# A keyed-expert stage: products of 512 columns, modulation sums moved to GpSimd, weights stored tile by tile

## What is computed

```
mod = jax.nn.silu(c) @ ada_w[l] + ada_b[l]
sh1, sc1, g1, sh2, sc2, g2 = jnp.split(mod[:, None, :], 6, axis=-1)
```

## Time and profile before

| | us |
|---|---|
| median of 3 runs (2588.99 to 2591.70) | 2591.24 |
| the profiled execution, its own time | 2591.11 |
| its span in the trace | 2589.3 |
| TensorE busy in the span | 2547.6 (98%) |
| VectorE busy | 1985.1 (77%) |
| ScalarE busy | 1426.9 (55%) |
| GpSimd busy | 0.2 (4 instructions) |

### The profile page before, as it was taken

How to read it: one execution, slowest core, us unless ns; L and a number is a source line. 1 busy time by engine, 2 the same in 40 slices (tenths; PEclk the granted TensorE clock), 3 DMA queues, 4 the chain that set the end, 5 groups by cost and what they waited for, 6 DMA issues and landing times. The chain is left out here.

```text
span 2589.3 us, 41783 instructions
## 1 busy us (share of the span) xinstructions
PE 2547.6 (98%) x14614; PEld 2210.2 (85%) x14614; DVE 1985.1 (77%) x2776; ACT 1426.9 (55%) x1835; POOL 0.2 (0%) x4
## 2 busy tenths in 40 slices
PE   9999999999999999999999999999999999999998
PEld 5798889897898888888889998878888888888887
DVE  6688378996787777776856645568988889898897
ACT  4654243484544444444544434457777777776775
POOL 0000000000000000000000000000000000000000
PEclk9999999999999999999999999999999999999999
DMA  8423345425787878786434555259999999999996
GB/s 340 159 98 105 116 131 169 137 81 188 242 312 282 299 280 278 249 297 203 154 113 141 184 181 170 97 210 381 343 349 351 349 360 347 361 356 344 353 357 225
DMA packets 223747, 627.19 MB, mean 242 GB/s; under 512 B 15344, under 2 KB 23568, under 8 KB 223376
## 3 DMA queue, kind: packets, MB, share of 16 engines
q1 hardware_dynamic: 223632, 625.64, 69.2%
HBM read 619.29 MB, written 6.29 MB: 242 GB/s over the span
## 5 line engine op out<-in xcount | busy, mean ns | idle before, releaser
L3870 DVE TENSOR_TENSOR wide_low<-wide,wide_high 128x2048 fp32r<-128x2048 f32 x288 | 657.4, 2288 | 97.8 <-ACT wide_high L3745 95.9
L3745 ACT ACTIVATE wide_high<-wide 128x2048 fp32r<-128x2048 f32 x288 | 552.5, 1919 | 210.3 <-PE bank L3597 104.4
L232 DVE TENSOR_TENSOR expert_tile_low<-slot,expert_tile_high 128x1024 fp32r<-128x1024 f32 x216 | 263.6, 1223 | 119.9 <-ACT expert_tile_high L224 119.9
L224 ACT ACTIVATE expert_tile_high<-slot 128x1024 fp32r<-128x1024 f32 x216 | 227.3, 1054 | 182.2 <-PE bank L242 65.7
L3593 PE MATMUL bank<-wide_high,xg_high 128*128 128x512 f32 x768 | 302.8, 394 | 0.1
L3594 PE MATMUL bank<-wide_high,xg_low 128*128 128x512 f32 x768 | 299.5, 390 | 0.0
L3597 PE MATMUL bank<-wide_low,xg_high 128*128 128x512 f32 x768 | 205.6, 389 | 0.0
L241 PE MATMUL bank<-h_high,expert_tile_high 128*128 128x256 f32 x704 | 173.4, 284 | 0.0
L242 PE MATMUL bank<-h_low,expert_tile_high 128*128 128x256 f32 x704 | 172.6, 283 | 0.0
L3597 PEld LDWEIGHTS bank<-wide_low,xg_high 128*128 128x128 f32 x768 | 144.1, 188 | 30.4
L3593 PEld LDWEIGHTS bank<-wide_high,xg_high 128*128 128x128 f32 x768 | 144.3, 188 | 29.4 <-DVE xg_low L3822 0.9
(11 more groups left out here) (611 smaller groups left out, 5133.4 us busy)
## 6 DMA issues: line engine op xcount, KB each, us to landing
wide<-in_moe_gu SPq DMA_DIRECT2D x192, 1024.0 KB, 6.4
wide<-in_moe_d SPq DMA_DIRECT2D x96, 1024.0 KB, 7.0
slot<-in_peer_u SPq DMA_DIRECT2D x128, 512.0 KB, 4.4
slot<-in_peer_v SPq DMA_DIRECT2D x128, 512.0 KB, 4.5
slot<-in_w_in SPq DMA_DIRECT2D x72, 512.0 KB, 3.6
picked_or_ada<-in_ada_w SPq DMA_DIRECT2D x48, 512.0 KB, 5.1
ada_slot<-in_ada_w SPq DMA_DIRECT2D x48, 512.0 KB, 4.7
slot<-in_ffn_gu SPq DMA_DIRECT2D x48, 512.0 KB, 3.6
```

Source lines behind the costliest of these rows:

```text
L224: core.nc.scalar.activation(self.tile_hi[:, place % 2], core.slot[u][:], ACT.Copy).then_inc(self.hi_ready.sem, 1)
L232: core.nc.vector.tensor_tensor(self.tile_lo[:, place % 2], slot[:], self.tile_hi[:, place % 2].bitcast(F32), ALU.subtract)\
L3745: nc.scalar.activation(w_hi[n % NB][:].rearrange("p c n -> p (c n)"), wide[n % U][:], ACT.Copy).then_inc(hi_ready.sem, 1)
L3870: nc.vector.tensor_tensor(w_lo[n % NB][:].rearrange("p c n -> p (c n)"), wide[n % U][:], w_hi[n % NB][:].rearrange("p c n -> p (c n)").bit ...
```

## The change

1. `Split` puts h's high and low parts side by side, so that for each block of 128 rows the 256 high columns and the 256 low ones are one run of 512.
2. A new `products_of_both` has 8 products of the high tile with these 512 columns and 8 of the low tile with the 256 high ones. A bank then holds two sums of 256 columns which somebody has to add. It is used for u's tiles in `experts` and for the gate and up tiles in `feed_forward`.
3. In `experts` VectorE adds the two halves (`sum_halves`, a reduce of 128x512 into `act_g`), once for each tile of u, and the gelu then reads `act_g` in place of the bank.
4. `add_tile` goes from VectorE to GpSimd as two instructions: `tensor_scalar` of the landed tile in place, and `tensor_tensor` that adds it to the sums (the first tile of a strip has only the `tensor_scalar`). There are two sums in turn, and four landing places in place of two. `add_rows` comes up to two rounds after the strip's last tile.
5. `weights` is laid out as [partition, tile, token]. What is used up of it makes the room for two of the landing places and for the second sums. `weigh` then reads 256 values in a run; the copy in `spread_weights` reads its bank with a stride and writes runs of 4.
6. In `feed_forward` VectorE adds the halves of every gate and up bank (two more reduces for a pair of tiles), and multiplies out of memory in place of the bank.

```diff
-        self.high, self.low = (core.sb(ctx, f"{name}_{part}", [P, C, n], F32R) for part in ("high", "low"))
+        self.parts = core.sb(ctx, f"{name}_parts", [P, C, 2, n], F32R)
+        self.high, self.low = self.parts[:, :, 0, :], self.parts[:, :, 1, :]
...
+    def products_of_both(self, pe, place, i, bank, split):
+        nc = self.core.nc
+        pe.wait_ge(self.hi_ready.sem, self.hi_ready.at(place + 1) + i * 4)
+        for c in range(C):
+            last = nc.tensor.matmul(bank[:, 0:2 * N], self.tile_hi[:, place % 2, c, :], split.parts[:, c].rearrange("p a n -> p (a n)"),
+                                    start=(c == 0), stop=False, skip_group_check=True)
+        last.then_inc(self.hi_used.sem, 1)
+        pe.wait_ge(self.lo_ready.sem, self.lo_ready.at(place + 3) + i * 4)
+        for c in range(C):
+            last = nc.tensor.matmul(bank[:, 0:N], self.tile_lo[:, place % 2, c, :], split.high[:, c, :], start=False, stop=(c == C - 1),
+                                    skip_group_check=True)
+        last.then_inc(self.core.tiles_used.sem, 1)
...
-            weights = core.sb(cg, "weights", [P, N, P])
+            weights = core.sb(cg, "weights", [P, P, N])
...
-                nc.scalar.activation(weights[:, q * B:q * B + B, :], core.bank[k % W][:, :].rearrange("p (b n) -> p b n", n=P), ACT.Copy)\
+                nc.scalar.activation(weights[:, :, q * B:q * B + B], core.bank[k % W][:, :].rearrange("p (b n) -> p n b", n=P), ACT.Copy)\
...
+    SLOTS = 4
-    slots = (side, core.sb(ctx, "ada_slot", [P, D]))
-    acc = core.sb(ctx, "ada_sums", [P, D])
+    slots = (side, core.sb(ctx, "ada_slot_1", [P, D]), within(0, "ada_slot_2", [P, D]), within(4, "ada_slot_3", [P, D]))
+    acc = (core.sb(ctx, "ada_sums_0", [P, D]), within(8, "ada_sums_1", [P, D]))
...
-                    if t >= 2:
-                        sp.wait_ge(summed.sem, summed.at(t - 1))
-                    if t > 1 and t % C == 1:
-                        sp.wait_ge(column.sem, column.at(t // C))
-                    sp.dma_start(slots[t % 2][:], ada[t]).then_inc(side_landed[t % 2].sem, 16)
+                    if t >= SLOTS:
+                        sp.wait_ge(summed.sem, summed.at(t - SLOTS + 1))
+                    sp.dma_start(slots[t % SLOTS][:], ada[t]).then_inc(side_landed[t % SLOTS].sem, 16)
...
-                halver.products(pe, place, i, lambda c: core.bank[w][:, 0:N], lambda c: split.high[:, c, :], lambda c: split.low[:, c, :])
+                halver.products_of_both(pe, place, i, core.bank[w], split)
...
+            sum_round = lambda t: t // 3 if t < 3 * THREES else (t - THREES) // 2
+            rows_due = {sum_round(g * C + C - 1) + 2: g for g in range(S)}
...
-            def add_tile(t, g=0):
...
+            def sum_halves(w, j, k):
+                dve.wait_ge(used.sem, used.at(E + k) + j * 4)
+                nc.vector.tensor_reduce(act_g[:, w, :], core.bank[w][:, :].rearrange("p (a n) -> p n a", a=2), AX.X, ALU.add).then_inc(u_summed.sem, 1)
+
+            def round_(j):
                 for w in range(2):
                     dve.wait_ge(geled.sem, geled.at(w + 2) + j * 2)
                     weigh(w, E + w, act_g[:, w, :], j * 2 + (E + w), j * 2)
-                    if tiles[w]:
-                        add_tile(tiles[w][0], g)
                     dve.wait_ge(used.sem, used.at(E + 2 * w - 1) + j * 4)
                     act_to_low(w, E + w, j * 2)
                     lower(2 + 2 * w, j + B0)
-                    if len(tiles[w]) == 2:
-                        add_tile(tiles[w][1], g)
+                    sum_halves(1 - w, j, 2 * w + 2)
                     lower(3 + 2 * w, j + B0)
...
+        @block.gpsimd
+        def _(pool):
+            for t in range(SIDE):
+                g, c, w = t // C, t % C, t % SLOTS
+                pool.wait_ge(side_landed[w].sem, side_landed[w].at((16 * (GROUPS // 2) if w < 2 else 0) + 16 * (t // SLOTS + 1)))
+                if c == 0:
+                    if g >= 2:
+                        pool.wait_ge(column.sem, column.at(g - 1))
+                    ins = nc.gpsimd.tensor_scalar(acc[g % 2][:], slots[w][:], core.c2s[:, c, :], None, ALU.mult)
+                else:
+                    nc.gpsimd.tensor_scalar(slots[w][:], slots[w][:], core.c2s[:, c, :], None, ALU.mult).then_inc(scaled.sem, 1)
+                    pool.wait_ge(scaled.sem, scaled.at(t - g))
+                    pool.wait_ge(summed.sem, summed.at(t))
+                    ins = nc.gpsimd.tensor_tensor(acc[g % 2][:], slots[w][:], acc[g % 2][:], ALU.add)
+                ins.then_inc(summed.sem, 1)
```

More of the change, by code:

```diff
@@ L1621, in retrieval @@
                     spread_weights(core, c2, a, h, picked, side[:, 3 * N:4 * N], weights, stage, early)
-            experts(core, cg, a, weights, split, side, early)
+            experts(core, cg, a, weights, split, side, early, within)
         core.release("keys_loaded", "keys_scored", "choose_vector_steps", "choice_exp", "choice_ready", "choice_turned", "choice_kept", "scores_kept",
@@ L2003, in zero_banks, with experts @@
         core.nc.tensor.matmul(core.bank[b][:, :].rearrange("p (o n) -> p o n", o=4), core.zeros[:], core.zeros[:].rearrange("p (o n) -> p o n", o=1).broadcast_to([P, 4, P]), start=True, stop=False, skip_group_check=True)
-def experts(core, ctx, a, weights, split, side, early):
+def experts(core, ctx, a, weights, split, side, early, within):
     nc = core.nc
     E = EARLY
+    SLOTS = 4
     act_g = core.sb(ctx, "act_g", [P, 2, N])
@@ L2023, in experts @@
     halver = Halver(core, ctx, "expert")
-    side_landed = [core.count(f"ada_landed_{w}") for w in range(2)]
+    side_landed = [core.count(f"ada_landed_{w}") for w in range(SLOTS)]
+    u_summed, scaled = core.count("expert_halves_summed"), core.count("ada_rows_scaled")
     stored = [core.count(f"early_stored_{k}") for k in range(STAGES)]
@@ L2116, in add_rows @@
             def add_rows(g):
-                pe.wait_ge(summed.sem, summed.at(C) + g * C)
+                pe.wait_ge(summed.sem, summed.at(C * g + C))
                 if g == 0:
@@ L2163, in _ @@
             dot(E, 0, 0)
-            for j in range(THREES):
-                round_(j, rows_in(j))
-            for j in range(THREES, PAIRS - 1):
-                k = j - THREES
-                round_(j, (k // 4 + (3 * THREES // C - 1), None) if k % 4 == 0 and k <= TWOS else (None, None))
+            for j in range(PAIRS - 1):
+                round_(j)
             turn_rows()
@@ L2251, in weigh @@
                 dve.wait_ge(weighed.sem, weighed.at(n - 1) + i) if not isinstance(n, int) or n >= 2 else None
-                row = weights[:, :, bass.ds(tile, 1)].rearrange("p t o -> p (t o)")
+                row = weights[:, bass.ds(tile, 1), :].rearrange("p o t -> p (o t)")
                 nc.vector.tensor_tensor(act_g[:, w, :], source, row, ALU.mult).then_inc(weigh_steps.sem, 1)
@@ L3378, in gate_and_up @@
                         pe.wait_ge(free.sem, free.at(u // 2 + 1) + i * 2)
-                    halver.products(pe, u, i, lambda c: core.bank[u][:, 0:N], lambda c: split.high[:, c, :], lambda c: split.low[:, c, :])
+                    halver.products_of_both(pe, u, i, core.bank[u], split)
             def down_part(i, u):
@@ L3442, in round_ @@
                     halver.lower(dve, place + u, i)
+                    if u == 0 and before is not None:
+                        gate_sum(1, before)
                     if u == 1 and before is not None:
                         hidden(1, before)
+                    if u == 2 and here:
+                        gate_sum(0, i)
                     if u == 3 and here:
@@ L3483, in feed_forward @@
     rescaled.passed(3)
+    for count in (gate_summed, hid_high):
+        count.passed(FT - 2)
     halver.passed(U * R, False)
```

129 lines of the change are left out of this document (62 added, 67 removed).

## The result

The changed kernel takes 2692.62 us (median of 4 runs, 2691.24 to 2694.86), the kernel before 2590.11 on the same chip (4 runs, 2587.68 to 2591.7): a ratio of 1.0392, interval 1.0380 to 1.0405. It is slower by 102.5 us. The prediction was 2710.

The account below looks back on a forecast made before the run. TensorE was taken as the bound, busy 2547.6 of 2589.3 us. To 2591.1 came +90.2 and +52.8 for GpSimd's turns, -0.6, -9.7, -10.8, +0.5 and -3.1: +119.3, so 2710 us, range 2568 to 2800.

Parts of the forecast that it names:

- Wide products: TensorE's products of u, gate and up: 0.07 us gained a tile, 6.2 on 88 tiles, 3.1 in the feed-forward part.
- Adding the halves: VectorE's reduces, 0.69 us each: hidden in the rounds and feed-forward part, 0.5 us later at the end.
- Weights tile by tile: Strided copy out of a bank before the rounds: taken as no cost, at most 23.7 us; `weigh` 0.42 for 0.62.
- Landing places: Four places for modulation tiles: the first 16 rounds' 9.7 us of gaps go; SyncE's queue now waits for sums.
- The sums on GpSimd: GpSimd's price for a modulation tile: scaling 1.5 us, addition 2.22, together 3.44; ends 1.82 and 4.16.
- One at a time: In the rounds, GpSimd and VectorE's two-input instructions (3.28 us a half) exclude each other: 2710 us, chance 0.62.
- The sum: Half a round of `experts` takes 8.44 us with three tiles (+90.2 in all), 6.72 with two (+52.8).
- The rule of turns: In the rounds, VectorE's 3.28 us of two-input instructions and GpSimd's tile work add up in each half.
- The signs it named: Profile signs in the rounds: L233 lengthened from 1.21 us, TensorE waiting for `act_lo`, or GpSimd over 3.7 us a tile.
- the slow rival: In the rounds, no mutual blocking, but GpSimd's 4.16 us a tile delays SyncE's queue: 2589.8 us; 0.09 with slow copies.
- side by side, but GpSimd is slow: Three-tile rounds take 12.5 us for 11.24 through SyncE's queue, +19.8: 2589.8 us; chance 0.09 shared with slow copies.

Follow-up runs that it names:

- e6_on_vector_narrow: Changed kernel with the sums back on VectorE and u's high products narrow again (16 of 256 columns): 2583.47 us, ratio 0.9969.
- e5_on_vector: Changed kernel with the modulation's sums back on VectorE as one fused instruction a tile, the rest kept: 2569.13 us, ratio 0.9915.
- e7_on_vector_two: Changed kernel with the sums back on VectorE and two landing places in place of four: 2570.29 us, ratio 0.9917.
- e3_add_only: Changed kernel with GpSimd's addition in full, its scaling on one column, first tiles filled: 2733.15 us with a ninth round, stage 563.6.
- e2_scale_only: Changed kernel with GpSimd's scaling in full and its addition on one column: 2570.47 us, ratio 0.9918, stage 503.8.
- e8_two_scalings: Changed kernel with a second full scaling on GpSimd in place of the addition: 2661.06 us, ratio 1.0276, stage 590.9.
- e1_tiny: Changed kernel with GpSimd's scaling and addition on one column, first tiles filled: 2677.36 us with a ninth round, stage 503.5.

## Why the prediction was nearly right, and where it was not

The time, 2692.6, lies 17 us under the forecast and in its range, the sign was the likeliest one, and the place (the rounds, L233 and `act_lo` lengthened, 1.21 and 0.41 us as their shortest) was named. But two of its steps were off in opposite directions, and the nearness is luck in that part: with the prices that GpSimd really has, its own rule gives 2854 us, above its range of 2568 to 2800.

- **Wide products**: right mechanism, size a little low. A half of a round went from 5.62 to 5.51 us (predicted 5.55), a feed-forward tile from 2.88 to 2.79. With `e6_on_vector_narrow` the two are worth 14.3 us together; 9.3 had been put down.
- **Adding the halves**: right. The reduces take 0.68 us (L2277, L3465) against 0.69 predicted from L3215, and the part after the stage became 2.9 us shorter, so they are hidden there.
- **Weights tile by tile**: right. The strided copy takes 596 ns (L1971) where it took 597, and `weigh` 0.42 us where nothing disturbs it (`e5_on_vector`).
- **Landing places**: the gaps are gone as predicted, in `e5_on_vector` the clock is 1.00 from 715 on and TensorE busy 284.3 of 285 us. The cause was named wrongly: with two places all but some 3 us of the gain stays (`e7_on_vector_two`). By the traces it is rather the sums in tiles of their own, which is not shown. The wait that comes in, SyncE's for the sums, is there with 251.4 us, and it is the main path of the loss: TensorE waits 60.4 us for tiles against 20.2 for `act_lo`. The prediction named this path, but its sum priced only VectorE's turns.
- **The sums on GpSimd**: the mis-sized term. The addition takes 2.34 at its shortest and 2.44 on the mean against 2.22. The scaling takes 2.84 at its shortest and 3.75 on the mean, against 1.5 chosen and 2.22 as the upper end: the bound itself was wrong. It was taken from instructions of VectorE, as if GpSimd at its slowest needed no more for one input than VectorE for two. A tile is 6.2 us, not 3.44. The Trainium skill, GPSIMD Engine Reference, section Engine selection, gives about twice VectorE's time for two inputs and roughly line-rate for one. For two inputs this trace agrees, 2.40 against 1.22 us. For one it does not: 2.84 against 0.75 us (L2283 before), so the measurement decides.
- **One at a time**: half right. For additions it holds: 3.02 for 1.22 us, 2.34 for 0.42, and 60 us when they stand alone (`e3_add_only`). For scalings it holds in part. A scaling waits, at its start, for a VectorE instruction that is under way (4.08 us in place of 2.84 in the period shown, 1.24 for a single column), and holds VectorE's two-input ones for 0.97 us (`e2_scale_only`). In its last 1.88 us they run in their normal time. This is also where the 0.69 us of `act_lo` in that period come from: the scaling ends at 1121.79, its last 1.88 us begin at 1119.91, and 0.42 later, at 1120.33, `act_lo` ends. The Trainium skill, SBUF — State Buffer, section Who interferes with whom, calls it an exclusive lock, which whoever issues first has for the whole instruction. The additions (2.34 us for 0.42) agree with it, the scalings (0.97 of 2.85 us) do not.
- **The sum**: 8.44 and 6.72 us were predicted for a half with three and two tiles in its round; measured are 8.06 (720.89 to 978.87, 32 halves) and 6.58 (to 1294.49, 48 halves). The rule of turns with the true prices, 2.84 + 7/8 x 2.40 = 4.94 us a tile, would have given 3.28 + 1.5 x 4.94 = 10.7 and 8.2 us, a time of 2854 with the other terms as they stood. The price too low and the rule too wide cancelled.
- **The signs it named**: two of them came together. L233 has a mean of 1508 ns, the sign for one at a time, and GpSimd needs 5.4 us for a tile in the rounds with three (258.0 / 48), with SyncE waiting for sums, the sign for the slow rival.
- **The rival "side by side, but GpSimd is slow"** had the mechanism that does most: its limit of 3.70 us for a tile in a round of three, passed through SyncE's queue. At the 564 us of work measured it gives 564 - 455 = 109 of the 120 us by which the changed kernel's stage exceeds that of `e5_on_vector`; GpSimd's waits for VectorE are in these 564 us. It came out at 2589.8 because its highest price for a tile, 4.16 us, had the same too low bound in it.

What is shown: a pace of some 6.1 us a tile costs 87 us with hardly a wait of TensorE for VectorE (`e8_two_scalings`), holding by additions alone 60 (`e3_add_only`), without either the stage is within 1 us of the best (`e1_tiny`), and both together cost 120. They overlap, because a scaling lengthened by its wait is also pace. The two parts of the stage help to tell them apart. At its shortest prices GpSimd's work for the 48 tiles of the rounds with three is 42 x 5.18 + 6 x 2.84 = 235 us, an estimate from 2.84 and 2.34 us, and they last 183 in `e5_on_vector`: some 52 of the 75 us lost there are pace without any disturbance. The 48 tiles of the rounds with two need the same 235 us and have 272. There pace alone should cost little (9 us in `e8_two_scalings`, at 6.1 us a tile), so most of the 44 us lost would come from the two engines lengthening each other's instructions. That split is worked out and was not tried.

Open is how the remaining 11 us over GpSimd's count come about. TensorE's mean clock was 0.93 from 715 to 1000 us, where it waited for tiles, against 1.00 in `e5_on_vector`; how much of the 11 us is the clock was not separated. Nor do the runs say why a scaling holds VectorE for its first 0.97 us alone and an addition for nearly all of its length.

## What to carry to other kernels

Before work is given to an idle engine, count that engine's own time for all of it against the stretch it must fit, with prices of that engine and not of another; here at least 469 us (96 tiles at the shortest prices), and 564 as it came, had to fit into 455. Count it stretch by stretch, since three tiles in a round did not fit and two would have. Then look at which queue waits for it: SyncE's one queue turned a slow side job into late weights for TensorE. A fused two-input instruction on a VectorE that is 90% busy, 1.28 us, was cheaper than 5.2 us on an engine that has nothing else to do.

When an experiment changes values, look first whether a loop's count hangs on them; then compare stages, not totals.

## What was unexpected of the hardware

- GpSimd scales 128x1024 in 2.84 us and fills it in 0.96, so the writing is the smaller part. Its one-input scaling is slower than its two-input addition (2.34 to 2.40 us).
- A scaling by GpSimd held VectorE's two-input instructions out in its first 0.97 us and not in its last 1.88.
- An addition of 512 columns took 1.27 us undisturbed but 1.95 on the mean, where one of 1024 took 2.34 and 2.44: the shorter ones met a low part under way more often.
- One column scaled by GpSimd took 0.28 us undisturbed and 1.24 when it began during one of VectorE's low parts, with `weigh` right behind.
